# Cached keys turned on VectorE in 32x32 blocks, and scores from sixteen row and column tiles, in a hybrid attention decoder step

## The reference

```python
x = LN1(alpha*x + 0.5*gate1 * SwiGLU_1(mod1(x)))
x = LN2(alpha*x + gate2 * W_o [mixA(h) ; mixB(h)])        # h = mod2(x), one projection h @ w_qkv for both mixers
x = LN3(alpha*x + 0.5*gate3 * SwiGLU_2(mod3(x)))
```

```python
s = einsum('bqhce,bkhce->bhcqk', q, k_cached_and_new) * e**-0.5     # mixer B; mixer A alike with its key set
attn = softmax(s[:, :, 0]) - lam * softmax(s[:, :, 1])
out  = attn @ v
```

## Time and profile before

| | |
|---|---|
| median of 3 runs | 1683.74 us (1680.97 to 1686.27) |
| profiled execution, its own time | 1686.0 us, span 1684.2 us |
| TensorE busy | 1534.2 us, 91% of the span |
| VectorE busy | 667.2 us, 40% |
| ScalarE busy | 513.7 us, 31% |
| granted TensorE clock over the span | 0.958 |

### The profile page before, as it was taken

How to read it: one execution, slowest core, us unless ns; L and a number is a source line. 1 busy time by engine, 2 the same in 40 slices (tenths; PEclk the granted TensorE clock), 3 DMA queues, 4 the chain that set the end, 5 groups by cost and what they waited for, 6 DMA issues and landing times.

```text
span 1684.2 us, 31988 instructions
## 1 busy us (share of the span) xinstructions
PE 1534.2 (91%) x12575; PEld 1341.7 (80%) x12575; DVE 667.2 (40%) x1333; ACT 513.7 (31%) x835; POOL 66.1 (4%) x162
## 2 busy tenths in 40 slices
PE   4899999999998999888898878877899999999996
PEld 3788999999996777655565555547789999999996
DVE  0322323322426423354554545645643232332343
ACT  2411222221214121244444444443342222221122
POOL 0200000000002000000000000000010000000000
PEclk9999999999998999989999999988989999999998
DMA  9993232232222141478888998873212222233211
GB/s 331 389 333 123 75 87 78 84 99 86 72 71 83 50 131 63 123 218 264 264 264 270 256 273 246 271 228 96 73 45 81 87 75 87 77 99 86 85 54 57
DMA packets 215906, 245.71 MB, mean 146 GB/s; under 512 B 9023, under 2 KB 152889, under 8 KB 215810
## 3 DMA queue, kind: packets, MB, share of 16 engines
q1 hardware_dynamic: 215810, 244.42, 46.9%
HBM read 237.31 MB, written 7.08 MB: 145 GB/s over the span
## 4 chain that ended last, share of the span: by engine, by line
PE 40%; SPq 8%; issue 3%; DMA 3%; DVE 3%; ACT 2%; ACTq 0%; DVEq 0%
PE ps L288 27%; SPq L1170 4%; SPq L1147 4%; PE ps L1256 3%; DMA kv<-in_cache_diff_k_dram 3%; PE ps L272 2%; PE ps L1268 1%; PE ps L1312 1%; PE ps L1330 1%; PE ps L952 1%; PE ps L1355 1%; PE ps L1295 1%; DVE VH L1571 1%; DVE xT L312 1%; DMA kv<-in_cache_win_v_dram 0%
## 5 line engine op out<-in xcount | busy, mean ns | idle before, releaser
L257 ACT ACTIVATE whi<-w 128x1024 fp32r<-128x1024 f32 (+1 forms) x152 | 171.1, 1128 | 741.5 <-PE ps L288 641.9
L263 DVE TENSOR_TENSOR wlo<-w,whi 128x1024 fp32r<-128x1024 f32 (+1 forms) x152 | 200.4, 1319 | 422.3 <-ACT whi L257 422.0
L288 PE MATMUL ps<-hhi,whi 128*128 128x288 f32 x1440 | 310.7, 297 | 3.7 <-ACT tmp L653 3.7
L288 PE MATMUL ps<-hlo,whi 128*128 128x288 f32 x1440 | 308.9, 296 | 0.0
L288 PE MATMUL ps<-hhi,wlo 128*128 128x288 f32 x1440 | 308.7, 296 | 0.0
L288 PEld LDWEIGHTS ps<-hhi,whi 128*128 128x128 f32 x1440 | 232.2, 189 | 9.2 <-issue 4.8
L288 PEld LDWEIGHTS ps<-hlo,whi 128*128 128x128 f32 x1440 | 232.8, 189 | 0.0
L288 PEld LDWEIGHTS ps<-hhi,wlo 128*128 128x128 f32 x1440 | 232.5, 189 | 0.0
L1256 PEld LDWEIGHTS ps<-ident,kv 128*128 128x128 f32 (+1 forms) x896 | 101.7, 149 | 88.9 <-issue 65.4
L1256 PE MATMUL ps<-ident,kv 128*128 128x128 f32 (+1 forms) x896 | 126.1, 283 | 46.0 <-DMA kv<-in_cache_diff_k_dram 33.2
L288 PE MATMUL ps<-ffhi,whi 128*128 128x288 f32 x704 | 151.2, 296 | 0.0
(11 more groups left out here) (197 smaller groups left out, 1684.8 us busy)
## 6 DMA issues: line engine op xcount, KB each, us to landing
w<-in_ffn_w_in_dram SPq DMA_DIRECT2D x88, 512.0 KB, 3.8
wada<-in_w_ada_dram SPq DMA_DIRECT2D x18, 2048.0 KB, 13.8
kv<-in_cache_diff_k_dram SPq DMA_DIRECT2D x128, 256.0 KB, 4.0
kv<-in_cache_diff_v_dram SPq DMA_DIRECT2D x128, 256.0 KB, 3.6
w<-in_ffn_w_out_dram SPq DMA_DIRECT2D x32, 704.0 KB, 4.6
w<-in_w_qkv_dram SPq DMA_DIRECT2D x24, 512.0 KB, 3.7
kv<-in_cache_win_k_dram SPq DMA_DIRECT2D x32, 384.0 KB, 5.1
kv<-in_cache_win_v_dram SPq DMA_DIRECT2D x32, 384.0 KB, 7.6
```

The lines of the kernel that those rows point to most:

```text
L257: nc.scalar.activation(whi[:, slot, 0:w], w32[:, slot, 0:w], ACT.Copy).then_inc(ph.hi, 1)
L263: nc.vector.tensor_tensor(wlo[:, slot, 0:w], w32[:, slot, 0:w], whi[:, slot, 0:w].bitcast(F32), ALU.subtract).then_inc(ph.lo, 1)
L288: m = pe.matmul(ps[:, banks + h, 0:TH], w, x[:, kk, h * TH:(h + 1) * TH], start=(kk == 0 and n == 0), stop=(kk == kall - 1 and n == 2))
```

## The change

1. **Keys.** `turn_keys` leaves TensorE. VectorE turns a whole load slot by one `transpose` instruction into `KC` (now tile by tile: up to 4 tiles x 512 columns), in 32x32 blocks: key 32a + t of column block 32j + e comes to stand at partition 32a + e, column 32j + t. It waits for the load (`k_landed`) and for the scores of the quarter before (`d_sc`). The evacuations on ScalarE (L1406) and VectorE (L1480) are gone. The key slot is free as soon as this one instruction is done.
2. **Scores.** For every 32-key group a of a tile and every f, four matmuls (cc = 0..3) over 32 feature rows each, on the array tile (32a, 32f), accumulate in PSUM bank a: 64 matmuls of 32 x nt columns in place of 4 (48 for the 96-key tiles). A tiny matmul (`carry_wait`) goes first and carries the wait.
3. **Queries.** Twice per sequence TensorE repeats the query blocks over the four partition groups (`spread_queries`, 16 matmuls) and VectorE copies them to `QR`.
4. **Maxima.** `top` becomes three or four instructions of `nt x 32` columns, one for each bank, and the final maximum is over the column block `tops`.
5. **Banks and order.** The scores take banks 0 to 3. The turned weights move to bank 7, the weights of the new keys to bank 4, and the prompt's weights times values and the RMS mean to bank 6, which they share with the prompt's turned weights; new waits keep these apart. `prompt_out` on VectorE goes ahead of `turn_keys` in its quarter; the square root of the RMS norm on ScalarE goes to the head of quarter 4.
6. **Projection.** `copy_turned` of a group's fifth tile goes behind the next group's first `split_hi`.

```diff
             for g in range(6): for c in range(4):      # qkv_scalar
                     if 4 * g + c >= 2:
                         split_hi(qkv, 4 * g + c, c % 2)
+                    if g - 2 in ROTS and c == 0:
+                        for t in TURNS[3]:
+                            copy_turned(g - 2, t)
...
-                if g - 1 in ROTS:
-                    for t in TURNS[3]:
-                        copy_turned(g - 1, t)
+            for t in TURNS[3]:
+                copy_turned(4, t)
...
-                pe.wait_ge(sem("d_kca"), 2 * q + 2)
-                pe.wait_ge(sem("d_kcv"), 2 * q + 2)
+                if c == 0:
+                    pe.wait_ge(sem("d_qr"), 2 * b + m + 1)
+                pe.wait_ge(sem("d_kt"), q + 1)
                 if positive(q):
-                    pe.wait_ge(sem("d_smax"), q)
-                for f in range(4):
-                    mm = pe.matmul(ps[32 * f:32 * f + 32, 2, 0:w], QB[:, m, f, :], KC[:, f, 0:w], start=True, stop=True,
-                                   tile_position=(0, 32 * f))
+                    pe.wait_ge(sem("d_smax"), tops_done(b, i))
+                carry_wait(0)
+                for cc in range(4):
+                    for f in range(4):
+                        for a in range(kw // 32):
+                            r = slice(32 * a, 32 * a + 32)
+                            mm = pe.matmul(ps[32 * f:32 * f + 32, a, 0:nt * 32], QR[r, m, cc, f, :],
+                                           KC[r, 0:nt, (4 * f + cc) * 32:(4 * f + cc + 1) * 32], start=(cc == 0), stop=(cc == 3),
+                                           tile_position=(32 * a, 32 * f))
                 mm.then_inc(sem("d_sc"), 1)
+            def spread_queries(b, i):
+                m = i // 4
+                pe.wait_ge(sem("d_qb"), 4 * b + 2 * m + 2)
+                if positive(QUARTERS * b + i):
+                    pe.wait_ge(sem("d_smax"), tops_done(b, i))
+                for cc in range(4):
+                    for a in range(4):
+                        mm = pe.matmul(ps[32 * a:32 * a + 32, 0, 64 * cc:64 * cc + 64], ident[:, 32 * cc:32 * cc + 32],
+                                       QB[:, m, :, 0:2 * NS], start=True, stop=True, tile_position=(0, 32 * a))
+                mm.then_inc(sem("d_spread"), 1)
...
+                if pm == 0 and i in (1, 5):            # prompt_turn
+                    heads = head_of(pm, b, i)
+                    if positive(heads):
+                        pe.wait_ge(sem("p_out"), heads)
...
-                pe.wait_ge(sem("p_copied"), PT_ * hd + PT_)
+                pe.wait_ge(sem("p_copied"), PT_ * hd + PT_ + ahead)      # prompt_values
...
-                eng.tensor_copy(KC[:, f, 0:w], ps[:, 1, 0:w]).then_inc(sem("d_kcv"), 1)
+                eng.wait_ge(sem(f"k_landed{c % 2}"), landed_at(b, m, c))
+                if positive(q):
+                    eng.wait_ge(sem("d_sc"), q)
+                eng.transpose(KC[0:kw, 0:nt, :].rearrange("p k e -> p (k e)"),
+                              kv(c % 2)[0:kw, 0:nt, :].rearrange("p k e -> p (k e)")).then_inc(sem("d_kt"), 1)
...
+                for a in range(kw // 32):              # top
+                    rows_of = lambda ap: ap.rearrange("p (k a t) -> p a k t", k=nt, t=32)[:, a]
+                    one = stat_at(m, c) + a
+                    eng.tensor_tensor_reduce(out=rows_of(S[m][:, o:o + w]), in0=ps[:, a, 0:nt * 32].rearrange("p (k t) -> p k t", t=32),
+                                             in1=rows_of(bias), scale=1.0, scalar=MASKED,
+                                             op0=ALU.add, op1=ALU.max, accum_out=tops[:, one:one + 1]).then_inc(sem("d_smax"), 1)
```

More of the change, by code:

```diff
@@ L182, in build @@
         assert o <= fend
+        QR, o = place("QR", [P, 2, 4, 4, 32], offset=o)
+        tops, o = place("tops", [P, NPAGE + 1], offset=o)
         kv23, o = place("kv23", [P, 2, 4, QW], offset=hreg)
@@ L1054, in chunk_keys, with stat_at, tops_done @@
             return CH[m][c] * keys_of(m, tile0(m, c))
+        def stat_at(m, c):
+            return sum(keys_of(m, tile0(m, k)) // 32 for k in range(c))
+        def tops_done(b, i):
+            m, c = divmod(i, 4)
+            return b * (stat_at(0, 4) + stat_at(1, 4)) + m * stat_at(0, 4) + stat_at(m, c)
         def landed_at(b, m, c):
@@ L1242, in attend_tensor @@
             pe.wait_ge(sem("vout"), 2 * (PT_ + 1))
[L1247 to L1257, removed]
@@ new lines, in scores, with carry_wait @@
+                mm.then_inc(sem("d_sc"), 1)
+            def carry_wait(bank):
+                pe.matmul(ps[0:32, bank, 3 * P:3 * P + 4], ident[:, 0:32], ident[:, 0:4], start=True, stop=True, tile_position=(0, 0))
+            def spread_queries(b, i):
[8 more added lines that the diff above has]
+                mm.then_inc(sem("d_spread"), 1)
@@ L1381, in body @@
                     tb, ti = back(b, i, 1)
-                    if alive(tb) and is_turn(mixer_of(tb, run), ti):
+                    turning = alive(tb) and is_turn(mixer_of(tb, run), ti)
+                    if turning:
                         prompt_turn(tb, ti, mixer_of(tb, run))
@@ L1545, in body @@
                             eng.tensor_tensor(QT[:, 4:8, cols], part[:], turned_o[:, :, 0:NS], ALU.add).then_inc(sem("d_out"), 1)
+                    hb, hi_ = back(b, i, 3)
+                    if alive(hb) and ends_head(mixer_of(hb, run), hi_):
+                        prompt_out(hb, hi_, mixer_of(hb, run))
+                    if alive(b):
+                        turn_keys(b, i)
+                    if alive(b) and c == 0:
+                        eng.wait_ge(sem("d_spread"), u + 1)
+                        src = ps[:, 0, 0:2 * P].rearrange("p (c f s) -> p c f s", c=4, f=4)
+                        eng.tensor_copy(QR[:, m, :, :, 0:2 * NS], src).then_inc(sem("d_qr"), 1)
                     if alive(b):
@@ L1560, in body @@
                             eng.wait_ge(sem("d_new"), u + 1)
-                            eng.reduce_max(stat[:, 36:37], S[m][:, o:o + NSM], AX_X).then_inc(sem("d_mnew"), 1)
-                    hb, hi_ = back(b, i, 3)
-                    if alive(hb) and ends_head(mixer_of(hb, run), hi_):
-                        prompt_out(hb, hi_, mixer_of(hb, run))
+                            eng.reduce_max(tops[:, stat_at(m, 4):stat_at(m, 4) + 1], S[m][:, o:o + NSM], AX_X).then_inc(sem("d_mnew"), 1)
                     if alive(b):
```

87 lines of the change are left out of this document (35 added, 52 removed).

## The result

The changed kernel takes 1795.87 us (median of 4 runs, 1795.2 to 1801.64) where the kernel before takes 1685.0 us beside it (1680.97 to 1686.27). The ratio is 1.0673, with a 95% interval of 1.0648 to 1.0697: 6.7% slower. The forecast was faster, 1670 us in a range of 1642 to 1755: the kernel became slower, and the time lies outside the range.

What follows compares the result with a forecast made beforehand. In attention no engine was full, stretches paced by TensorE and SyncE alternating; in QKV TensorE stalled between groups. Attention +2 and QKV -16 gave -14 us against the 1683.74 median: 1670 us, range 1642 to 1755.

Steps and rivals of the forecast that it cites:

- The later copy: QKV projection: the next group's first high part is ready earlier, removing TensorE's stalls between groups; -15.9 us.
- Turn: Attention: VectorE's new key-turning instruction, priced at 1.07 ns an element; 2.3 us, 1.2 for near keys.
- The slow and the fast turn: Rivals on VectorE's key turn: slow, each further ns an element costs 115 us, 1785, chance 0.10; fast, 0.52 ns, 1646, 0.10.
- Maxima: Attention, VectorE's top: one 0.69 us instruction becomes four at 0.28 plus 0.03 gap, 1.25 us; 0.95 in mixer A.
- Scores at 12.5 ns: Attention, TensorE: 128 score records a quarter at the fastest pace in the trace; 1.6 us, 1.2 for 96-key quarters.
- TensorE's scores (1.6) run beside the prompt's step as long as they stay under 2.0.: Attention cycle: scores hide beside VectorE's 2.0 us prompt work, so VectorE's queue makes a page quarter 5.7 us.
- the "0": Attention: spread_queries, small carry_wait matmuls and tile-shape changes lie beside VectorE's turn; 0, or +2 us where that cover fails.
- What was late next is now VectorE itself: Attention: VectorE, not SyncE's 48 us path, sets the sequence period; 50.5 us, 54.1 with the RMS norm.
- The rival that ended on this side: Attention scores at the old pace, 28 ns a record, stick out of the prompt's step; 1751 us, chance 0.16.
- the +2: Attention's total in the forecast sum, over sequence periods, first sequence, tail and cover; +2 us.
- A near quarter: Attention: VectorE's chain for a quarter of near keys; 4.4 us, two of them in a sequence's 42.4.
- The 1737 us: Kernel time estimated under the skill's rule that matmul starts never come closer than about 25 ns; scores 3.2 us a page quarter.

Runs made afterwards that it cites:

- wide kernel: The changed kernel with scores from 16 matmuls of 512 columns a quarter instead of 64 of 128, three quarters of the contraction left out; 1717.99 us.
- half of the turn: VectorE turns only half of each quarter's keys: 1792.87 us on the changed kernel, 1691.93 us on the wide kernel.
- the kernel with one full quarter: The wide kernel with the changed kernel's 64 score matmuls in quarter 5 alone; 1760.53 us, or 1755.92 us with TensorE's sequence loops written out.
- the kernel before written out: The kernel before with TensorE's loops over the sequences written out, same instructions; 1687.06 us, ratio 1.0021.
- twelve turns of four: The wide kernel plus 48 idle 4-column matmuls a quarter, run as a small hardware loop of four matmuls; 2036.67 us.

## Why the prediction was wrong

- *The later copy*, -15.9 us: right. The product of the projection became 15.8 us shorter, and the copy alone gives 18 (13.5 to 22.7).
- *Turn* 2.3 and 1.2 us: 2.30 and 1.24. The slow and the fast turn are both out; between the two sizes lie (2304-1244)/1024 = 1.04 ns an element, where 1.07 was forecast. The Trainium skill ("Vector Engine (DVE) Microarchitecture Reference", section 3.8) states one element per cycle per lane for that mode. The time per element is constant here, as that says; how long a cycle is no row here shows.
- *Maxima* at 0.28 a piece: 0.287. The four overlap: in the wide kernel what follows starts 0.85 us after the first of them (839.46 to 840.31 us), 1.25 were forecast.
- *Scores at 12.5 ns*: the pace of an undisturbed burst at 2.4 GHz is right, 1.64 us from the first to the last of 128 starts, 12.9 ns, and at 64 columns 128 records lie in 1.48 us. But of the 32 page quarters only 11 take 1.64 us. Without a stop at 1.2 GHz it is 2.4 us, more than the 2.0 under which the scores had to stay, and with stops it is up to 5.5. The Trainium skill ("TensorE: Matmul & The Clock Gate", Part 1) would have no start closer than about 25 ns; these runs of 128 disagree with it.
- *"TensorE's scores (1.6) run beside the prompt's step as long as they stay under 2.0."* This step failed, and with it the "0" for all that TensorE has to do beside VectorE's turn. I priced 256 instructions a quarter by how fast a burst of them starts, and named in a rival that they "must be fed" without asking from where. The loop over the sequences had stayed with the engine; with 2,770 instructions it does not, 11 to 13 packets a sequence are fetched, and TensorE stands still for 74 us with nothing else to wait for. Taking three quarters of the score matmuls away removes these stops and gives 78 us back. The profile before held the sign of it: 61 packets in all, none of them in the later turns of the first loop.
- *"What was late next is now VectorE itself"*: wrong for the changed kernel (half of the turn gives nothing that can be told from noise), half right without the stops (26 us of the 62 that the chain alone would have given). The wide kernel's 48 us over the forecast point to a second omission in the same step, which no run tests: the scores stand behind turned weights, prompt turn and values in TensorE's queue, and TensorE, with less to do and more to wait for, runs at its lower clock for part of the time (0.82 in the mean of a sequence against 0.93 to 0.99). How these two share the 48 us was not separated.
- *The rival that ended on this side* named the scores, at 1751 us, but by a slower pace per record; its mechanism did not occur. The range failed because it held only prices of instructions and none of their supply.
- *Its sums.* The terms for attention add up to +0.2; the +2 counts the failed cover, priced at 0 or +2, in full. A near quarter gives 4.3 us by the terms named, not 4.4. The 1737 us do not take off the 10 us that the 1751 take off; with them it is about 1730. None of this comes near the 126 us between forecast and result.
## What to carry to other kernels

Before many small matmuls replace few large ones inside a hardware loop, count the instructions of the loop's body and look at the instruction queue's packets in each turn of the kernel as it is: an engine that fetched nothing there may begin to fetch everything. The price does not show in the pace of a single burst. And when a change has independent hunks, time each alone: here the small one was worth 1.1%, and the rest cost 8%.

## What the runs showed of the hardware

- TensorE's instructions come in packets of 16 KB, 0.9 to 1.5 us each in most cases. In the kernel with one full quarter a loop body of 1,488 recorded instructions stays with the engine from its second turn on; one of 1,520 is fetched in each turn, with more packets than when it is written out (7 to 9 against 6 to 7).
- In the changed kernel 36 of TensorE's 40 waits that nothing else ends are over 1.3 to 1.7 us after a packet has landed. At low density (over 10 us for some 250 instructions, the kernel before written out) the packets cost nothing that shows.
- A turn of a small hardware loop on TensorE costs about 0.3 us beyond its matmuls at 2.4 GHz and 0.5 at 1.2 (twelve turns of four: 0.38 and 0.62 us a turn).
- Sixteen 32x32 tiles take matmul passes of 128 columns every 12.9 ns at 2.4 GHz, and 32 passes of 512 columns in 1.14 to 1.17 us. Passes of 4 columns on one and the same 128x32 tile with a weight load each start only every 32 ns, at 1.2 GHz every 53.
- VectorE turns 128x2048 float32 elements in 32x32 blocks in 2.30 us and 128x1024 in 1.24.
